# Filler products on the tensor engine in the opening of a two-block transformer kernel: 23 of 69 taken out

## The chip, the cores and the metric

The kernel runs on one core of a Trainium2 chip. The metric is the device time of one execution in microseconds (us), lower is better. Engines are called as in the profile: PE is the tensor engine's matmuls, PEld its weight loads, DVE the vector engine, ACT the scalar engine, POOL the GpSimd engine, SPq the queue from which the DMAs are issued. The "granted clock" of PE is 1.00 at 2.4 GHz and 0.50 at 1.2 GHz.

## The reference, cut to what matters

Two blocks of two layers each work on 256 tokens (the first block on 256 context tokens too) of width 1024. Each layer of the first block is modulated: a vector of 9 x 1024 numbers is computed from a condition vector and then scales and shifts the normed tokens before every sub-layer. The change lies before the very first sub-layer:

```python
mod_l = (jax.nn.silu(c) @ ada_w[i] + ada_b[i])[:, None, :]
sh1, sc1, g1, sh2, sc2, g2, sh3, sc3, g3 = jnp.split(mod_l, N_MOD, axis=-1)
x = x + 0.5 * g1 * swiglu(modulate(rms(x), sh1, sc1), pre_wi, pre_wo)
```

Only the first two parts, sh1 and sc1 (2 x 1024 numbers, for the latent and for the context condition), are needed before the first weight product of the feed-forward step. Everything behind that is the long rest: feed-forward, attention, and the second block.

## The kernel before, in words

**The stages.** The program is a list of stages, and each engine runs its part of each stage in the same order, held together by semaphores. The first stages are `statistics` (sum of squares of the tokens), `ada` (sh1 and sc1 on the tensor engine), `norm` (the modulated tokens, as a rounded high part `h_hi` and a rest `h_lo`), and the first feed-forward stage, which begins with `first_opening`.

**The ada stage.** The two weight parts come in eight pieces of 1 MB (512 rows by 512 columns each), one DMA each into a ring of four buffers `raw` (line 55, `RAWS = 4`). In `ada_step` (lines 923 to 941) a "row" step multiplies one piece by the condition, in 4 products of 512 columns that use 32 columns of the array each (line 935). After two pieces ACT copies the sums to `rows` (line 1415). After four pieces a "turn" step (line 940) brings the 1024 sums into the layout of the tokens, by 8 products of 2 columns. So `s.steps` holds ten steps: pieces 0 to 3, a turn, pieces 4 to 7, a turn. The first turn gives sh1, the second sc1; DVE adds the bias (line 2043) and one (line 2033).

**The filler.** `keep_awake(n)` (lines 956 to 959) multiplies a constant table of ones by itself, 128 columns, n times, into half of the bank `pm` that nobody reads. `ada` (lines 943 to 954) issues 28 of them before the first piece and then 5, 5, none (the square sums of line 787 stand there), 2, 2 (first turn), 5, 5, 5, 2, 10 (second turn) behind the ten steps. That is 69 calls. The profile counts each fp32 product twice (138 records at line 959, 8 per piece at line 935, 16 per turn at line 940).

**The loads.** SPq issues all loads in one order: a constant table, the tokens, the eight pieces, and then the weight units of the feed-forward step (2 DMAs of 512 KB each, all at line 706, in blocks of 512 bytes). Pieces 4 to 7 each wait until the piece that held their buffer has been multiplied; the units 0, 1, 2 and 3 wait in the same way for pieces 4, 5, 6 and 7:

```python
elif kind == "unit":
    sp.wait_ge(S["ada_done"], len(ada_units) - RAWS + n + 1)
```

**The first feed-forward products.** ACT rounds unit 0 to `w_hi` (line 1391), then makes `h_hi` of the first two of eight token chunks (line 1473), then rounds unit 1, then goes on with `h_hi`. DVE makes `full` (line 2102) and `h_lo` (line 2121) chunk by chunk. `first_opening` on PE takes a chunk as its `h_lo` comes: for the chunks 0 to 2 four products of unit 0 (lines 796 and 797), from chunk 3 on four of unit 0 and four of unit 1; then the products by the units' low parts (line 803), and the context tokens (lines 732 to 734).

Of the kernel before, what the change touches and what calls it, by code (L numbers as in the profile page):

```python
# [57 lines left out]
PER_MOD = (KC // ADA_K) * (D // ADA_COLS)  # L58
# [127 lines left out]
def build(nc, x_t, vecs, consts, positions, cond_rows, ada_first, ada_t, pre_wi, pre_wo, post_wi, post_wo, a_w_qkv, a_w_o, b_w_qkv, b_w_o,  # L186
# [413 lines left out]
    def con(name):  # L600
        if name in ANGLES:
            return angles[:, ANGLES.index(name), :]
        o, w = CON[name]
        return con_sb[:, o:o + w]
# [74 lines left out]
    with block:  # L679
# [36 lines left out]
        def _(pe):  # L716
# [63 lines left out]
            def square_sums(st, p):  # L780

                tok = st.parts[p]
                per = 0 if st.after is None else st.after.run.cols // P
                pe.wait_ge(S["square_added"], st.b["square_added"] + KC + 2 * per * p)
                if p:
                    pe.wait_ge(S["log_ready"], st.b["log_ready"] + p)
                pe.matmul(pm[:, 0, tok], con("ones"), square_sum[:, tok], start=True, stop=True).then_inc(S["square_summed"], 1)
# [135 lines left out]
            def ada_step(s, k):  # L923

                kind, j, bank_i, before = s.steps[k]
                o = ADA_BANKS[bank_i]
                if before is not None:
                    pe.wait_ge(S[before[0]], before[1])
                if kind == "row":
                    n = s.run.t0 + j  # L930
                    w, landing, count = raw_of("ada", n)
                    pe.wait_ge(landing, count)
                    for c in range(ADA_K):
                        quarter = slice(32 * c, 32 * (c + 1))
                        last = pe.matmul(o[quarter, :], cond[:, j % 2 * ADA_K + c, :], w[:, c * ADA_COLS:(c + 1) * ADA_COLS],
                                         start=j % 2 == 0, stop=j % 2 == 1)
                    last.then_inc(S["ada_done"], 1)
                    return
                for c in range(KC):
                    last = pe.matmul(o[:, 2 * c:2 * c + 2], rows[:, c * P:(c + 1) * P], con("fold"), start=True, stop=True)  # L940
                last.then_inc(S["ada_turned"], 1)

            def ada(s):
                pe.wait_ge(cond_ready, 1)
                pe.wait_ge(early_landed, 16)
                keep_awake(28)
                for k in range(len(s.steps)):
                    ada_step(s, k)
                    if k == 2:
                        square_sums(s.first, 0)  # L950
                    elif s.steps[k][0] == "turn":
                        keep_awake(10 if k + 1 == len(s.steps) else 2)
                    else:
                        keep_awake(2 if s.steps[k + 1][0] == "turn" else 5)

            def keep_awake(n):

                for _ in range(n):
                    pe.matmul(pm[:, 1, 0:P], con("ones"), con("ones"), start=True, stop=True)
# [400 lines left out]
            def branch_out(s):  # L1360
                waits_of(pe, s)
                sweep(pe, s.run, lambda u: dense(u, SEQ, x_of(s), s.ready))

            todo = dict(ada=ada, ffn_in=dense_run, proj=dense_run, heads=heads, values=values, diff=diff, soft=soft, pairs=pairs,
                        iw=iw, glu=dense_run, cc=cc, plain=plain, gates=gates, stick=stick,
                        branch=branch_out, conv_in=dense_run)
# [1682 lines left out]
```

## Time and profile before

| | |
|---|---|
| median of 3 runs | 2828.85 us |
| lowest and highest of them | 2827.34 and 2831.7 us |
| the profiled execution, its own time | 2830.01 us |
| its span, first to last instruction | 2827.9 us |
| PE busy | 2782.1 us, 98% of the span |
| mean granted clock of PE over the span | 0.998 |

The profile is of one execution. Its span is 2.1 us shorter than its time. Times in the views count from the start of the span. A busy PE is not PE at its peak, since the ends of pipelined matmuls are modelled; the pace is read from starts, or from the number of products in a stretch. The ada stage and the first products lie in the first 66 us.

### The profile page before, as it was taken

The page shows a single profiled execution, that of the slowest core. Times are in us where ns is not written, and L with a number is a line of the kernel's source. Part 1 is how long each engine was busy: PE and PEld are TensorE (multiplying, and loading weights), DVE is VectorE, ACT ScalarE, POOL GpSimd, SP SyncE. Part 2 cuts the span into 40 slices and gives each one's busy share as a digit, 9 for nine tenths or more (in the row PEclk, how much of TensorE's full clock was granted, in tenths as well). Part 3 has the DMA queues.
Part 4 walks back from the last instruction along what each step waited for, and adds up shares of the span by engine and source line. Part 5 has one row for each costly group of instructions (what it writes and reads, how often), then busy time and mean ns, then how long its engine had stood idle before and what let it go on. Part 6 is the DMA issues. An engine that isn't in the chain of part 4 may idle for free.

```text
span 2827.9 us, 43713 instructions
## 1 busy us (share of the span) xinstructions
PE 2782.1 (98%) x18332; PEld 2515.5 (89%) x18332; DVE 1994.0 (71%) x2863; ACT 1122.8 (40%) x1448; POOL 547.4 (19%) x408
## 2 busy tenths in 40 slices
PE   8999999989999999999999999999999999999999
PEld 7888897858888888888887999999999999999999
DVE  4767854386777858646577756988687788867866
ACT  4222234374212223122256435445553355455432
POOL 0100100000100101001000110798001129930000
PEclk9999999999999999999999999999999999999999
DMA  8656532202556635445331566554466675535665
GB/s 277 185 163 197 177 100 89 78 13 75 156 161 196 190 108 178 130 140 164 113 112 48 156 192 180 157 176 138 135 195 181 165 205 154 160 115 180 178 184 142
DMA packets 593171, 427.31 MB, mean 151 GB/s; under 512 B 16848, under 2 KB 571088, under 8 KB 592720
## 3 DMA queue, kind: packets, MB, share of 16 engines
q1 hardware_dynamic: 592976, 424.53, 50.7%
q8 instruction: 145, 2.38, 0.4%
q14 instruction: 50, 0.41, 0.0%
HBM read 423.43 MB, written 1.05 MB: 150 GB/s over the span
## 4 chain that ended last, share of the span: by engine, by line
PE 76%; POOL 13%; DVE 6%; DMA 2%; ACT 2%; issue 1%; SPq 0%; DVEq 0%; ACTq 0%; POOLq 0%
PE ps L732 22%; PE ps L733 22%; PE ps L734 21%; POOL cb_product L2919 7%; POOL cb_sum L2925 3%; DVE w_lo L1987 2%; ACT w_hi L1391 1%; DMA raw<-in_w_in 1%; PE ps L912 1%; PE ps L1056 1%; PE ps L1058 1%; PE ps L1057 1%; PE ps L913 1%; PE ps L914 1%; PE pm L1027 1%
## 5 line engine op out<-in xcount | busy, mean ns | idle before, releaser
L732 PE MATMUL ps<-h_hi,w_hi 128*128 128x256 f32 (+1 forms) x3488 | 1113.3, 319 | 7.3 <-DVE w_lo L1987 5.8
L733 PE MATMUL ps<-h_lo,w_hi 128*128 128x256 f32 (+1 forms) x3488 | 1105.4, 317 | 0.0
L734 PE MATMUL ps<-h_hi,w_lo 128*128 128x256 f32 (+1 forms) x3488 | 1105.3, 317 | 0.0
L1987 DVE TENSOR_TENSOR w_lo<-raw,w_hi 128x2048 fp32r<-128x2048 f32 (+2 forms) x376 | 813.4, 2164 | 231.2 <-ACT w_hi L1391 228.0
L1391 ACT CAST w_hi<-raw 128x2048 fp32r<-128x2048 f32 (+2 forms) x376 | 631.1, 1679 | 427.5 <-PE ps L734 299.8
L732 PEld LDWEIGHTS ps<-h_hi,w_hi 128*128 128x128 f32 x3488 | 665.5, 191 | 55.3 <-DVE w_lo L1987 8.3
L733 PEld LDWEIGHTS ps<-h_lo,w_hi 128*128 128x128 f32 x3488 | 665.8, 191 | 43.5 <-issue 0.2
L734 PEld LDWEIGHTS ps<-h_hi,w_lo 128*128 128x128 f32 x3488 | 665.7, 191 | 43.3
L2892 POOL TENSOR_TENSOR act_lo<-sil,act_hi 128x512 fp32r<-128x512 f32 (+1 forms) x132 | 164.9, 1249 | 1651.9 <-DVE act_hi L2262 1286.8
L732 PE MATMUL ps<-act_hi,w_hi 128*128 128x256 f32 (+1 forms) x1122 | 367.9, 328 | 0.7 <-DVE w_lo L1987 0.3
L733 PE MATMUL ps<-act_lo,w_hi 128*128 128x256 f32 (+1 forms) x1122 | 366.7, 327 | 0.0
L734 PE MATMUL ps<-act_hi,w_lo 128*128 128x256 f32 (+1 forms) x1122 | 366.6, 327 | 0.0
L2061 DVE SCALAR_TENSOR_TENSOR dot_t<-chunk_w,cond_all 128x1024 f32<-128x1024 f32 x256 | 310.4, 1258 | 6.4 <-DMA chunk_w<-in_ada_t 6.4
L1551 ACT ACTIVATE sil<-ps 128x512 f32<-128x512 f32 (+1 forms) x88 | 47.9, 544 | 557.9 <-PE ps L734 554.7
L732 PEld LDWEIGHTS ps<-act_hi,w_hi 128*128 128x128 f32 x1122 | 213.4, 190 | 20.3 <-DVE w_lo L1987 1.4
L733 PEld LDWEIGHTS ps<-act_lo,w_hi 128*128 128x128 f32 x1122 | 213.4, 190 | 18.1
L734 PEld LDWEIGHTS ps<-act_hi,w_lo 128*128 128x128 f32 x1122 | 213.4, 190 | 18.0
L2919 POOL TENSOR_SCALAR cb_product<-cb_in,vec_sb 128x256 f32<-128x256 f32 x120 | 195.1, 1636 | 5.9
L2159 DVE SCALAR_TENSOR_TENSOR xs<-ps,mod_sb,xs 128x256 f32<-128x256 f32 x136 | 60.5, 479 | 156.3 <-PE ps L734 156.3
L2260 DVE TENSOR_TENSOR sil<-sil,ps 128x512 f32<-128x512 f32 (+1 forms) x88 | 54.5, 619 | 142.4 <-ACT sil L1551 142.3
L2925 POOL TENSOR_TENSOR cb_sum<-cb_sum,cb_product 128x512 f32<-128x512 f32 x60 | 89.4, 1490 | 5.0
L1056 PE MATMUL ps<-w_hi,h_hi 128*128 128x256 f32 x288 | 82.8, 288 | 0.0
(312 smaller groups left out, 3178.8 us busy)
## 6 DMA issues: line engine op xcount, KB each, us to landing
chunk_w<-in_ada_t SPq DMA_DIRECT2D x128, 512.0 KB, 4.1
raw<-in_w_in SPq DMA_DIRECT2D x62, 1024.0 KB, 5.3
raw<-in_ffn_pre_wi SPq DMA_DIRECT2D x88, 512.0 KB, 5.3
raw<-in_ffn_post_wi SPq DMA_DIRECT2D x88, 512.0 KB, 5.2
raw<-in_ffn_pre_wo SPq DMA_DIRECT2D x32, 704.0 KB, 4.6
raw<-in_ffn_post_wo SPq DMA_DIRECT2D x32, 704.0 KB, 4.8
raw<-in_w_ffn_gate SPq DMA_DIRECT2D x44, 512.0 KB, 4.0
raw<-in_w_ffn_up SPq DMA_DIRECT2D x44, 512.0 KB, 5.3
```

The lines of the kernel that those rows point to most:

```text
L732: pe.matmul(o, hi, x_hi[:, k, tok], start=k == 0, stop=False)
L733: pe.matmul(o, hi, x_lo[:, k, tok], start=False, stop=False)
L734: return pe.matmul(o, weights(w_lo[u.low], u, k, m * P, P), x_hi[:, k, tok], start=False, stop=k == u.run.kc - 1)
L1056: pe.matmul(o, h_hi[:, k, tok], hi, start=k == 0, stop=False)
L1391: nc.scalar.copy(w_hi[u.slot][:, 0:n], whole[:, 0:n]).then_inc(hi_ready, 1)
L1987: nc.vector.tensor_tensor(w_lo[u.low][:, 0:n], whole[:, 0:n], w_hi[u.slot][:, 0:n].bitcast(F32), ALU.subtract).then_inc(lo_ready, 1)
L2061: nc.vector.scalar_tensor_tensor(dot_t[st], chunk_w[n % 2], 1.0, cond_all[:, st, :], ALU.mult, ALU.mult, accum_out=mod_sb[s.layer][:, at_f ...
L2159: last = nc.vector.scalar_tensor_tensor(xs[:, c, tok], o, mod_sb[layer][:, which * KC + c, st:st + 1], xs[:, c, tok], ALU.mult, ALU.add)
L2260: nc.vector.tensor_tensor(sil[:, r, 0:N], sil[:, r, 0:N], ps[u.slot][:, 1, 0:N], ALU.mult).then_inc(S[run.free], 1)
L2892: nc.gpsimd.tensor_tensor(o, whole, hi.bitcast(F32), ALU.subtract).then_inc(S[signal], 1)
L2919: ins = nc.gpsimd.tensor_scalar((product if w else dst)[:, c, :], x, weights_of(c, w), None, ALU.mult)
L2925: nc.gpsimd.tensor_tensor(dst[:, chunks, :], dst[:, chunks, :], product[:, chunks, :], ALU.add).then_inc(S[signal], 1)
```

## The change

The rule that says how many filler products stand behind a step is rewritten:

```diff
                     ada_step(s, k)
                     if k == 2:
                         square_sums(s.first, 0)
-                    elif s.steps[k][0] == "turn":
-                        keep_awake(10 if k + 1 == len(s.steps) else 2)
-                    else:
-                        keep_awake(2 if s.steps[k + 1][0] == "turn" else 5)
+                    elif k + 1 == len(s.steps):
+                        keep_awake(4)
+                    elif s.steps[k][0] == "row" and s.steps[k][1] + 1 < PER_MOD:
+                        keep_awake(5)
+                    elif s.steps[k + 1][0] == "turn":
+                        keep_awake(2)
```

`PER_MOD` is 4, the pieces of one part. Behind the ten steps there now stand 5, 5, the square sums, 2, 0, 0, 0, 0, 2 and 4 calls. The 28 before the first piece stay.

## Rows read from the trace of the kernel before

**Rows 1.** The page: busy time, then the chain that ended last

```profile
PE 2782.1 (98%) x18332; PEld 2515.5 (89%) x18332; DVE 1994.0 (71%) x2863; ACT 1122.8 (40%) x1448; POOL 547.4 (19%) x408
PE 76%; POOL 13%; DVE 6%; DMA 2%; ACT 2%; issue 1%; SPq 0%; DVEq 0%; ACTq 0%; POOLq 0%
```

**Rows 2.** Chain, 20 to 50 us: start us, length us, what

```profile
34.65 6.52 DMA raw<-in_ffn_pre_wi
41.19 1.90 ACT w_hi L1391
43.53 0.50 DVE h_lo L2121
```

**Rows 3.** Timeline of PE: start us, length us, operation, count [idle before]

```profile
23.89 1.07 PE L935 MATMUL ps<-raw,cond 128*32 128x512 f32 x8 [2.13 <-DMA raw<-in_ada_first]
...
27.47 0.69 PE L959 MATMUL pm<-con_sb 128*128 128x128 f32 x4
28.09 1.07 PE L935 MATMUL ps<-raw,cond 128*32 128x512 f32 x8
29.09 1.38 PE L959 MATMUL pm<-con_sb 128*128 128x128 f32 x10
30.40 1.07 PE L935 MATMUL ps<-raw,cond 128*32 128x512 f32 x8
...
32.70 1.07 PE L935 MATMUL ps<-raw,cond 128*32 128x512 f32 x8
...
35.01 1.07 PE L935 MATMUL ps<-raw,cond 128*32 128x512 f32 x8
...
36.78 1.95 PE L940 MATMUL ps<-con_sb,rows 128*128 128x2 f32 x16
38.59 3.97 PE L959 MATMUL pm<-con_sb 128*128 128x128 f32 x20
42.21 0.56 PE L796 MATMUL ps<-h_hi,w_hi 128*128 128x256 f32 x1
...
44.08 0.39 PE L796 MATMUL ps<-h_hi,w_hi 128*128 128x256 f32 x1 [0.44 <-DVE h_lo L2121]
```

**Rows 4.** Timelines of DVE and ACT, 38 to 45 us, columns as before

```profile
38.77 0.17 DVE L2043 TENSOR_TENSOR mod_sb<-ps,vec_sb 128x16 f32<-128x16 f32 x1 [10.88 <-PE ps L940]
...
39.90 0.90 ACT L1473 ACTIVATE h_hi<-full,mod_sb 128x256 fp32r<-128x256 f32 x2
41.19 1.90 ACT L1391 CAST w_hi<-raw 128x2048 fp32r<-128x2048 f32 x1 [0.39 <-DMA raw<-in_ffn_pre_wi]
```

**Rows 5.** Piece 5's issue; unit 1's; landing times of pieces 4 to 6, 7

```profile
18.06 0.37 SPq L706 DMA_DIRECT2D raw<-in_ada_first  x1
25.02 0.37 SPq L706 DMA_DIRECT2D raw<-in_ada_first  x1
31.52 3.08 SPq L706 DMA_DIRECT2D raw<-in_ffn_pre_wi  x1
...
raw<-in_ada_first SPq DMA_DIRECT2D x3, 1024.0 KB, 11.2
raw<-in_ada_first SPq DMA_DIRECT2D x1, 1024.0 KB, 9.7
```

**Rows 6.** Stretches: busy time of the engines, granted clock, DMA share, GB/s

```profile
35.00:36.00 1.00, 1.00 (x9) 0.16 (x8) 0.00 (x0) 0.00 (x0) 0.00 (x0) 1.00 0.78 209
37.00:38.00 1.00, 1.00 (x11) 1.00 (x10) 0.00 (x0) 0.00 (x0) 0.00 (x0) 1.00 0.63 174
...
8.70:39.30 30.60, 26.54 (x206) 17.57 (x205) 5.81 (x12) 9.03 (x15) 0.00 (x0) 1.00 1.04 361
39.35:42.70 3.35, 3.35 (x18) 3.35 (x17) 2.97 (x7) 2.96 (x4) 0.00 (x0) 0.50 1.04 300
```

**Rows 7.** PE near 2554 us: an idle stretch, then pace at either clock

```profile
2554.38 0.39 PE L732 MATMUL ps<-h_hi,w_hi 128*128 128x256 f32 x1 [2.73 <-DVE w_lo L1987]
...
2554.94:2558.34 3.40, 3.40 (x18) 3.40 (x17) 3.35 (x3) 0.00 (x0) 0.00 (x0) 0.50 0.54 172
2558.40:2561.80 3.40, 3.40 (x30) 3.40 (x30) 2.05 (x3) 1.91 (x1) 0.00 (x0) 1.00 0.00 0
```

**Rows 8.** All waits of PE from 45 to 564 us; filler pace

```profile
PE ps L796 <- DVE h_lo L2121: 0.2, 1, 0.2
...
4.80:8.30 3.50, 3.50 (x16) 3.50 (x17) 1.00 1.00 318
9.00:12.50 3.50, 3.50 (x34) 3.50 (x33) 1.00 1.05 400
```

## The prediction, made before the changed kernel was run

> **What bounds the kernel now.** I read the page first: PE is busy for 98% of the span and carries 76% of the chain [rows 1]. So what the opening does to the total is how much earlier or later PE begins its unbroken stream of products, provided nothing behind takes the shift back. I asked for PE's waits next: from 45 to 564 us there is one, of 0.2 us, at the very start [rows 8]. A shift of the stream passes on whole for 500 us, and I take it to pass on to the end, since the later stages hang on PE's products in turn.
>
> Then I asked what starts that stream. The timeline of PE shows it at 44.08 us, after 0.44 us of idling for `h_lo` [rows 3]. The eight products before that (chunks 0 and 1, from 42.21) are a prelude. The chain says what the stream waited for [rows 2]: the second DMA of unit 1, issued at 34.65 and landed at 41.17; ACT's rounding of unit 1, 1.90 us from 41.19; only then ACT's `h_hi` of chunk 2 and DVE's `h_lo` at 43.53. The filler behind the last turn, 3.97 us from 38.59 [rows 3], stands on no link of this. The reader should see that the wait that ends last at 44.08 is a landing, 0.39 us after ACT was free for it [rows 4].
>
> **The sum, part by part.** One filler call at full clock costs 0.26 us: the ten records from 29.09 end where piece 5 begins at 30.40, 1.31 us for five calls [rows 3]. At half clock it costs about twice that, 16 records in 3.5 us against 34 [rows 8].
>
> *Two calls behind the first turn, gone:* 27.47 to 28.09, 0.62 us. Piece 4 can start at 27.47 if it is there. The DMAs of pieces 4 to 6 took 11.2 us each, so piece 5, issued at 18.06, landed at 29.26, and its neighbours, read 2.71 us earlier and later, at 26.55 and 31.97 [rows 5]. Piece 4 is there. It ends near 28.5 in place of 29.1.
>
> *Fifteen calls behind pieces 4, 5 and 6, gone:* 3 x 1.31 = 3.9 us of PE time. But piece 5 lands at 29.26 (it started at 30.40), piece 6 at 31.97 (started 32.70), piece 7, issued at 25.02 with 9.7 us on the way, at 34.7 (started 35.01) [rows 3, 5]. PE waits for each in place of multiplying ones. Of 4.5 us removed, the last piece gains 0.3 us. The turn follows it, and DVE's bias (38.77) and the end of ACT's first two `h_hi` (40.80) come 0.3 us earlier [rows 4]. ACT then waits 0.7 us for unit 1 where it waited 0.4. Cost nothing, gain nothing, and the cover is that landing.
>
> *Does the landing move?* The units' DMAs wait for pieces 4, 5 and 6, and these end 0.5, 1.1 and 0.7 us earlier. Nothing is queued behind them on SPq that PE needs before 44 us but the units themselves. Unit 1's first issue started at 31.52 and stood for 3.08 us, to 34.60, just where piece 7 landed [rows 5]; the queue was full, not late, and an earlier start ends at the same place. The bound for a gain is what the DMA engines left unused: 0.22 us in 35 to 36 and 0.37 us in 37 to 38 [rows 6], 0.6 us together. The bound for a loss is unit 0's blocks getting between piece 7's, at most by the 0.5 us that they come earlier; that stays inside the 0.7 us of ACT's wait. I take nothing, because the issue row shows the full queue, and keep 0.6 us as the gain end.
>
> *Six calls behind the last turn, gone:* the filler ends near 39.4 at full clock in place of 42.56. Chunks 0 and 1 can start as their `h_lo` come, near 40.7 and 41.6, and are done by about 42.1; chunk 2 still comes at 44.02. Gain nothing.
>
> *What the filler held up:* the clock. It stood at 1.00 from 8.70 to 39.30 with PE busy for 26.5 of 30.6 us, among it an idle stretch of 2.13 us before piece 3, and fell to 0.50 from 39.35 to 42.70, directly after the stretch with the turn's two-column products. There PE worked without a pause at half clock, and the clock came back before the stream [rows 3, 6]. Now PE will do about 1 us of products between 39.4 and 44.08. The nearest row for what that does is at 2554 us: 2.73 us idle, then half clock over 3.40 us, in which 18 products ran where 30 run at full clock [rows 7]. That costs 3.40 x 12/30 = 1.36 us if all of it falls on the stream. The other end is 0: the half clock may be over by 44.08, as it was before, or lie on the prelude. Nothing in the trace says where it starts, so I take the middle, 0.7 us.
>
> *The rest of the diff* is Python, unrolled at build time. Sum: 0 + 0 + 0.7 = +0.7 us on the profiled execution's 2830.01 us, so 2830.7. The median of the three runs is 1.16 us below that execution, so 2829.6.
>
> **The rivals.** *No shift (28%).* The same chain, with the clock back in time or never down. For it: the half clock of before cost nothing, and 2.13 us of idling left the clock alone [rows 3, 6]. 2828.9 us.
>
> *A little faster (12%).* The earlier starts of the units' DMAs fill the unused 0.6 us, unit 1 lands 0.6 us earlier, and ACT is ready for it. Against it: the 3.08 us issue that ends with piece 7's landing [rows 5]. 2828.3 us.
>
> *Slower, by the clock among the pieces (13%).* From piece 4 on PE does 1.07 us of work in every 2.71 us and waits for a DMA in between; before, filler stood in all of these gaps. If the clock falls there and is at half through piece 7 and the second turn, piece 7 takes 1.0 us more and the turn 2.0 us more (its weight loads run at the filler's pace, and 16 records to 34 is a factor of 2.1) [rows 3, 8]. Less the 0.7 us that ACT waits for unit 1, the link is 2.3 us late, and 1.4 us at half clock behind it make 3.7 us: 2832.6 us. It decides once the turn ends over 0.7 us late. Two more stretches at half clock in the stream (2.7 us) would bring it to 6.4 us, 2835.3, over the bound for slower; I give that 4% of the 13. Against it stand the piece before 23.89, behind 2.13 us of idling, with no fall [rows 3, 6], and that PE at half clock is busy most of the time on the same pieces, after which it came back at 42.70.
> The Trainium skill speaks against the change here: "TensorE: Matmul & The Clock Gate", section "Loop structure matters more than you think", has it that a loop which waits for a DMA before each matmul runs at half clock. By that rule the pieces would all run so and the time would be this rival's, 2832.6 us; the trace agrees for the 2.73 us near 2554 us and not for the 2.13 us before piece 3.
>
> *The change doesn't do what it says.* By the conditions, steps 0 and 1 keep 5, step 3 and 8 keep 2, step 9 gets 4, the others nothing: 23 calls less. I give this nothing.
>
> **How the numbers follow.** Forecast 42%, no shift 28%, faster 12%, clock among the pieces 13%, and 5% for what I have not seen. The three runs of before alone span 2827.34 to 2831.7. The low end is the faster rival less the 1.5 us by which the lowest run lies under the median, 2826.8; the high end is the slower rival, 2832.6. About 0.2% of the time, 5.7 us, is what a measurement of this kernel can tell from no change. All cases but the longest clock case lie inside: slower 6% (4% and half of the unseen), faster 3%, the same 91%.
>
> **What would show it.** Line 959 has 92 records in place of 138. Pieces 5, 6 and 7 start at about 29.3, 32.0 and 34.75, each with idle time before it put down to `in_ada_first`. Unit 1's rounding still starts near 41.2 with ACT idle before it by about 0.7 us, and the product of chunk 2 near 44.1. The granted clock of the stretch 44 to 48 decides between forecast and no shift: below 1.00 and fewer than 8.3 products per us is the forecast. If unit 1's rounding starts before 40.9 the queue was not full and the faster rival holds. If the second turn lasts over 2.5 us the slower one does. A shift of the stream that PE makes up before 564 us would prove the first paragraph wrong.

## The result, and the profile after

The changed kernel takes 2835.62 us (median of 16 runs, 2833.36 to 2838.54), the kernel before beside it 2829.86 us (16 runs, 2827.28 to 2833.84). The ratio is 1.0019, 95% interval 1.0011 to 1.0027: slower by 5.8 us, 0.2%. The forecast was 2829.6 us and no difference, the range ended at 2832.6. The profiled execution took 2834.84 us, with a span of 2832.7 us, 4.8 us longer than before.

The page first, as [rows 1]:

```profile
PE 2782.6 (98%) x18286; PEld 2512.0 (89%) x18286; DVE 1993.6 (70%) x2863; ACT 1122.7 (40%) x1448; POOL 547.2 (19%) x408
PE 75%; POOL 13%; DVE 6%; DMA 3%; ACT 2%; issue 2%; SPq 0%; DVEq 0%; ACTq 0%; POOLq 0%
```

PE has 46 records fewer, the 23 calls, and is no less busy. The timeline of PE in the opening answers to [rows 3] (start us, length us, operation, count, idle before):

```profile
27.07 1.21 PE L935 MATMUL ps<-raw,cond 128*32 128x512 f32 x8
28.85 1.94 PE L935 MATMUL ps<-raw,cond 128*32 128x512 f32 x8 [0.57 <-DMA raw<-in_ada_first]
31.65 1.93 PE L935 MATMUL ps<-raw,cond 128*32 128x512 f32 x8 [0.87 <-DMA raw<-in_ada_first]
34.29 1.94 PE L935 MATMUL ps<-raw,cond 128*32 128x512 f32 x8 [0.70 <-DMA raw<-in_ada_first]
36.16 1.22 PE L961 MATMUL pm<-con_sb 128*128 128x128 f32 x4
37.17 3.41 PE L940 MATMUL ps<-con_sb,rows 128*128 128x2 f32 x16
40.45 2.05 PE L961 MATMUL pm<-con_sb 128*128 128x128 f32 x8
42.95 0.55 PE L796 MATMUL ps<-h_hi,w_hi 128*128 128x256 f32 x1 [0.46 <-DVE h_lo L2123]
...
45.42 0.39 PE L796 MATMUL ps<-h_hi,w_hi 128*128 128x256 f32 x1 [0.41 <-DVE h_lo L2123]
```

The pieces start when they land, as forecast, but the clock falls among them: a piece takes 1.94 us in place of 1.07 and the second turn 3.41 in place of 1.95. The stretches of the clock answer to [rows 6], ACT's and DVE's rows to [rows 4]:

```profile
11.00:27.80 16.80, 14.27 (x110) 8.73 (x108) 5.45 (x9) 6.64 (x12) 0.00 (x0) 1.00 1.05 388
27.90:44.90 17.00, 14.40 (x64) 8.46 (x60) 3.41 (x10) 6.23 (x8) 0.00 (x0) 0.50 1.08 328
```

```profile
40.62 0.17 DVE L2045 TENSOR_TENSOR mod_sb<-ps,vec_sb 128x16 f32<-128x16 f32 x1 [13.20 <-PE ps L940]
...
41.74 0.91 ACT L1475 ACTIVATE h_hi<-full,mod_sb 128x256 fp32r<-128x256 f32 x2 [2.00 <-DVE full L2104]
42.55 1.88 ACT L1393 CAST w_hi<-raw 128x2048 fp32r<-128x2048 f32 x1
```

ACT no longer waits for unit 1; unit 1 waits for ACT. Its rounding starts at 42.55 in place of 41.19, and the stream at 45.42 in place of 44.08: 1.34 us late. The clock is back at 44.9, just before it.

That is 1.34 of the 4.8 us by which the span grew. To find the rest I matched the two traces product by product on PE, from the end backwards, and took the difference of their starts:

| time in the kernel before, us | later in the changed kernel by, us |
|---|---|
| 45 to 345 | 1.35 |
| 370 to 1000 | 2.71 to 2.73 |
| 1060 to 1480 | 4.11 |
| 1600 | 5.16 |
| 1660 | 6.64 |
| 1780 | 7.15 |
| 2320 to 2500 | 7.93 |
| 2560 to the end | 4.73 to 4.87 |

The shift is handed on unchanged for 300 us and then grows in steps, the four largest of 1.0 to 1.5 us, far from anything that was edited.

The fall at 2554 us is time that the profile of the kernel before lost, not time that the change gained. PE's wait of 2.73 us there [rows 7] hangs on one load, in the chain of the kernel before (start us, length us, what):

```profile
2543.05 6.95 DMA raw<-in_w_in
```

In each of the 13 other profiles of this document that load takes 5.1 to 5.5 us, no half clock follows, and the kernel makes up 3.0 to 3.3 us on the kernel before; in the changed kernel the wait is 1.01 us. Only one profile of the kernel before was kept, so whether that kernel often loses these 3 us stays open. The shift of 4.7 us at the end is 7.9 less 3.2 of them.

The first step, in PE's waits from 45 to 564 us, as [rows 8]:

```profile
PE ps L732 <- POOL act_lo L2894: 1.1, 1, 1.1
PE ps L796 <- DVE h_lo L2123: 0.6, 2, 0.4
```

The wait of 1.1 us was not there. Followed back, in the changed kernel: PE waits at 353.53 for POOL's `act_lo`, POOL for DVE, and DVE for a chunk of the later modulation weights (line 691):

```profile
353.53 0.50 PE L732 MATMUL ps<-act_hi,w_hi 128*128 128x512 f32 x1 [1.07 <-POOL act_lo L2894]
```

```profile
346.97 1.23 DVE L2063 SCALAR_TENSOR_TENSOR dot_t<-chunk_w,cond_all 128x1024 f32<-128x1024 f32 x1 [2.95 <-DMA chunk_w<-in_ada_t]
```

The same load in the kernel before:

```profile
344.11 1.23 DVE L2061 SCALAR_TENSOR_TENSOR dot_t<-chunk_w,cond_all 128x1024 f32<-128x1024 f32 x1 [1.43 <-DMA chunk_w<-in_ada_t]
```

The load is issued 1.34 us later but lands 2.86 us later. The DMA view over its flight shows what was different. Changed, issue to landing (341.76 to 346.95), the last number of the row for `chunk_w` being us to landing:

```profile
q1 hardware_dynamic: 1469, 1.20, 78.2%
q8 instruction: 1, 0.02, 1.1%
...
chunk_w<-in_ada_t SPq DMA_DIRECT2D x1, 512.0 KB, 5.2
```

Before (340.42 to 344.09):

```profile
q1 hardware_dynamic: 655, 0.79, 74.0%
...
chunk_w<-in_ada_t SPq DMA_DIRECT2D x1, 512.0 KB, 3.7
```

In the changed kernel one 16 KB block of instructions (0.02 MB on queue 8, at 344.65 us) is fetched on the DMA engines while the load is on its way, and before there was none. The other large steps have the same shape, with a block at 1000.4 us (a load of 5.6 us against 4.2), at 1579.3 us (6.3 against 5.3) and at 1643.3 us (6.4 against 4.7).

Why would a block come later? In the kernel before two fetches in a plain stretch come at 188.0 and 216.4 us, and between them PE does 127 matmuls, each with its weight load:

```profile
188.00:216.40 28.40, 28.40 (x127) 23.54 (x126) 19.10 (x27) 5.37 (x4) 0.00 (x0) 1.00 0.65 200
```

So a block is PE's, some 256 of its instructions. The 23 calls were 92 instructions (46 matmuls, 46 weight loads). With them gone PE reaches every block boundary 46 matmuls further on in the work, 46 x 28.4/127 = 10.3 us later. The fetches, put on the clock of the kernel before (less the shift of PE at that place), stand at 331.8 and 360.5 before, and at 343.3 and 371.2 after, 11.5 and 10.7 us later. The Trainium skill ("Runtime: NRT & Kernel Launch", section "Instruction fetch mechanics") says that instructions are refilled in blocks of 16 KiB, 256 instructions each, by the sequencer's own DMA queue; the counts here agree. It adds that the cost of crossing a block is mostly hidden; no run here tests that for PE's own issue, but the loads beside it are another matter.

### The profile page after: what moved, and what is told of

The parts are those of the page before. It is cut to its first block, busy times and chain, and to the rows that moved or that the text cites. A ratio compares the mean times of both kernels' runs of the same rounds, so it can differ in the third digit from the quotient of the medians.

```text
span 2832.7 us, 43621 instructions
## 1 busy us (share of the span) xinstructions
PE 2782.6 (98%) x18286; PEld 2512.0 (89%) x18286; DVE 1993.6 (70%) x2863; ACT 1122.7 (40%) x1448; POOL 547.2 (19%) x408
## 4 chain that ended last, share of the span: by engine, by line
PE 75%; POOL 13%; DVE 6%; DMA 3%; ACT 2%; issue 2%; SPq 0%; DVEq 0%; ACTq 0%; POOLq 0%
PE ps L732 21%; PE ps L734 21%; PE ps L733 21%; POOL cb_product L2921 7%; POOL cb_sum L2927 3%; DVE w_lo L1989 2%; ACT w_hi L1393 1%; DMA raw<-in_ada_first 1%; DMA raw<-in_w_in 1%; PE ps L912 1%; PE ps L1058 1%; PE ps L1060 1%; PE ps L1059 1%; PE ps L914 1%; PE ps L913 1%
## 5 line engine op out<-in xcount | busy, mean ns | idle before, releaser
L732 PEld LDWEIGHTS ps<-act_hi,w_hi 128*128 128x128 f32 x1122 | 213.3, 190 | 24.4 <-POOL act_lo L2894 3.4
```

The lines of the kernel that those rows point to most:

```text
L732: pe.matmul(o, hi, x_hi[:, k, tok], start=k == 0, stop=False)
```

## The experiments

Three theories went into the first runs: the clock among the pieces (the slower rival of the prediction), the idle tail behind the last turn, and the position of the code. Most kernels have the rule replaced by a list of the ten counts behind the ten steps; in the diffs the minus line gives, in the same form, the counts of the kernel that it starts from. "Later part" below is the time from PE's first product at line 803, which ends the prelude and the first part of the stream, to PE's last, in the profiled execution: 2770.96 us before, 2774.38 changed. Both ends are starts of products. The start of that part is 51.32 before and 52.67 changed. Medians of a kernel are of 11 runs, those of the kernel before of the runs beside it on the same chip. A ratio and its 95% interval are as recorded, and need not be the quotient of the two medians. A profile is one of the 11 executions, and can lie some us from the median.

**Four calls in place of ten behind the last turn, alone.**

```diff
-                        keep_awake((5, 5, 0, 2, 2, 5, 5, 5, 2, 10)[k])
+                        keep_awake((5, 5, 0, 2, 2, 5, 5, 5, 2, 4)[k])
```

> The kernel before with one part of the change: 4 filler calls in place of 10 behind the last turn. Three theories. 'Among the pieces': the clock falls because PE idles between pieces 4 to 7, the second turn then runs at half clock and comes late; then this kernel is like the one before (about 2829.9 us, within 1.5) and its second turn still takes about 1.9 us. 'Tail': the idle stretch behind the last turn keeps the clock at half into the stream of products; then this kernel carries most of the 5.8 us (2834 to 2836) and the granted clock behind 44 us is below 1.00. 'Code position': every call taken out shifts the rest of the program on PE and the loads meet it differently; then it carries 6 of 23 calls' share, about +1.5 us, with the start of the stream unchanged.

2831.27 us against 2830.44, ratio 1.0002 (0.9993 to 1.0010). No theory of a large cost in the tail survives. The profile does show the clock at half well into the stream,

```profile
42.85:49.55 6.70, 5.95 (x26) 5.69 (x27) 5.89 (x14) 4.55 (x8) 0.00 (x0) 0.50 1.03 400
```

and the part from line 803 began at 54.22 us, 2.9 us late. But this kernel began badly too (half clock from 15.5 to 18.9 and 29.1 to 32.5, where all its filler stood), and the next but one shows the same with the tail whole.

**No calls behind pieces 4, 5 and 6, alone.**

```diff
-                        keep_awake((5, 5, 0, 2, 2, 5, 5, 5, 2, 10)[k])
+                        keep_awake((5, 5, 0, 2, 2, 0, 0, 0, 2, 10)[k])
```

> The kernel before with one part of the change: no filler calls behind pieces 4, 5 and 6 (15 calls less). 'Among the pieces': this is the part that costs, +3 to +6 us (2833 to 2836), piece 7 takes 1.9 us in place of 1.07 and the second turn 3.4 in place of 1.95. 'Tail': like before, within 1.5 us. 'Code position': 15 of 23 shares, +3.8 us, but with the start of the stream near 44.1 us.

2831.19 us against 2830.44, ratio 0.9999 (0.9990 to 1.0008). The turn does take 3.4 us, half clock from 32.7 to 42.9, and line 803 begins 1.0 us late (52.35). The forecast of the first theory, 3 to 6 us, is missed; that of the third, 3.8 us, as well, and with it the idea that the cost goes by shares of the calls. The later part is short, 2768.51 us, but the profiled execution, 2828.54 us, is the fastest of the 11.

**No calls behind the first turn, alone.**

```diff
-                        keep_awake((5, 5, 0, 2, 2, 5, 5, 5, 2, 10)[k])
+                        keep_awake((5, 5, 0, 2, 0, 5, 5, 5, 2, 10)[k])
```

> The kernel before with one part of the change: no filler calls behind the first turn (2 less). 'Among the pieces' and 'tail': no difference, within 1.5 us of before, since the filler behind piece 4 is there. A variant of 'among the pieces': the fall is decided at the first turn already (in the changed kernel the clock fell at 27.9 us, just behind it), then this kernel's granted clock falls near 28 us in the profile as well, and comes back sooner, since the filler behind pieces 4 to 6 keeps PE busy. 'Code position': +0.5 us.

2829.18 us against 2830.44, ratio 0.9995 (0.9986 to 1.0004). The clock did not fall near 28 us, so the variant of the theory misses. It fell later, with all the filler of before behind the pieces and the last turn:

```profile
44.55:51.25 6.70, 6.00 (x28) 6.00 (x29) 6.43 (x11) 2.46 (x6) 0.00 (x0) 0.50 1.01 399
```

28 products in 6.7 us, and line 803 at 54.73 us, 3.4 us late, in a kernel with one of the lowest medians of all (its profiled execution took 2832.14 us, 3.0 over the median). One profile of the opening is one draw: where the clock falls differs from execution to execution.

**The changed kernel with ten calls behind the last turn.**

```diff
-                        keep_awake((5, 5, 0, 2, 0, 0, 0, 0, 2, 4)[k])
+                        keep_awake((5, 5, 0, 2, 0, 0, 0, 0, 2, 10)[k])
```

> The changed kernel with 10 calls behind the last turn again. 'Among the pieces': nearly as slow as the changed kernel, 2833 to 2836 us, second turn 3.4 us long. 'Tail': back at 2830 us. 'Code position': 17 of 23 shares, +4.3 us, with the stream starting near 44.1 us.

2830.30 us against 2830.44, ratio 0.9997 (0.9988 to 1.0006). Six calls more and the 5.8 us are gone. Yet the six alone cost nothing (first run). Either the parts cost only together, or it is the number: 17 calls fewer is harmless and 23 is not. The later part is 2768.57 us, in an execution of 2828.43 us, 1.9 under the median.

The next four kernels tell these two apart, by calls at a place that is far from pieces 4 to 7 and the tail: the 28 ahead of the first piece.

**The changed kernel with 34 calls ahead, 17 fewer in all.**

```diff
-                keep_awake(28)
+                keep_awake(34)
```

> The changed kernel with 34 filler calls ahead of the first piece in place of 28: 17 calls fewer than before in all, the same number as in the kernel with ten calls behind the last turn, while pieces, turns and tail stay as changed. Theory 'code position': what cost 5.8 us is that with 23 calls fewer PE's instruction blocks of 16 KB are fetched some 10 us later against the stream of products, into loads that PE waits for (344.7, 1000.4, 1643.3 us in the changed kernel); with 17 fewer they come at 338.8 us on the clock of before again and miss them. Then this kernel is at 2829.5 to 2832 us, and the load issued near 341 us takes about 3.8 us in place of 5.2. Theory 'clock and tail together': the two parts cost only jointly, by the clock; then it is at 2834.5 to 2836.5 us like the changed kernel.

2829.73 us against 2830.31, ratio 0.9999 (0.9990 to 1.0008). The opening is the changed one in every row, with the turn at half clock,

```profile
33.97 1.94 PE L935 MATMUL ps<-raw,cond 128*32 128x512 f32 x8 [0.71 <-DMA raw<-in_ada_first]
35.84 1.23 PE L957 MATMUL pm<-con_sb 128*128 128x128 f32 x4
36.85 3.41 PE L940 MATMUL ps<-con_sb,rows 128*128 128x2 f32 x16
```

and the load near 341 us takes 4.1 us. The half clock even lasts longer, from 27.7 to 48.2 us, and line 803 begins at 53.31 us, 2.0 us later than before. The later part is 2768.65 us, 5.7 less than in the changed kernel, and the median is 5.6 us under the changed kernel's on this chip (2835.28 us, below), with no run of either among those of the other.

**The kernel before with 5 calls ahead, 23 fewer in all.**

```diff
-                keep_awake(28)
+                keep_awake(5)
```

> The kernel before with 5 filler calls ahead of the first piece in place of 28: all fillers of before around the pieces and turns stay, and 23 calls are gone, as in the change. 'Code position': from the stream's start to the end it takes as long as the changed kernel (from the first product at line 803 to the last some 2774 us, against 2768.5 to 2771.5 in the five others), there is PE idle time near 351 and 1007 us on the clock of before, and the time is 2833.5 to 2836.5 us. 'Clock and tail together': 2829 to 2832 us, unless the cold beginning makes the pieces late, which the start of the pieces would show.

2833.45 us against 2830.31, ratio 1.0009 (1.0000 to 1.0018), 0.05 us under the expected 2833.5 at the low end. The interval touches no difference, but the fastest of its 11 runs (2832.46) is slower than the slowest of the kernel with 34 ahead (2832.26). The opening is not quite that of before: with so few calls ahead the first piece runs at half clock (1.94 us), and line 803 begins at 51.75 us, 0.4 us late. Here the second turn runs at full clock,

```profile
37.70 1.95 PE L940 MATMUL ps<-con_sb,rows 128*128 128x2 f32 x16
```

and still the wait near 353 us and the late load are back, in PE's waits from 45 to 564 us and in the DMA view:

```profile
PE ps L732 <- POOL act_lo L2890: 1.2, 1, 1.2
...
chunk_w<-in_ada_t SPq DMA_DIRECT2D x1, 512.0 KB, 5.4
```

The later part is 2773.56 us. The same filler round the pieces as before, and 3.1 of the 5.0 us that the changed kernel is over the kernel before on this chip.

**The changed kernel with 21 calls ahead, 30 fewer in all.**

```diff
-                keep_awake(28)
+                keep_awake(21)
```

> The changed kernel with 21 filler calls ahead of the first piece: 30 calls fewer than before. 'Code position': the fetches move another 3.2 us back against the stream of products, near 346.5 us on the clock of before, behind the landing of the load near 345 that the changed kernel's fetch held up; the time changes again, with no change among pieces, turns and tail, by over 1 us in either direction (about 2831 to 2834 if the hits are narrow). 'Clock and tail together': the same as the changed kernel within 1 us, 2834.5 to 2836.5 us.

2832.11 us against 2830.31, ratio 1.0007 (0.9998 to 1.0015), 3.2 us under the changed kernel beside it. Seven calls less and it is faster. The time did move by over 1 us with pieces, turns and tail untouched, as the code position asks and the clock theory does not. The fetch stands at 345.5 us on the clock of before; the load has landed by then, in 3.6 us:

```profile
chunk_w<-in_ada_t SPq DMA_DIRECT2D x1, 512.0 KB, 3.6
```

**The changed kernel again.**

> The changed kernel, unchanged, on the chip and beside the runs of the three others: 2834.5 to 2836.5 us by every theory. 'Code position': a second profile has its fetch of 16 KB near 343.3 us on the clock of before and a late load there again, whatever its clock did in the opening. If the clock in the opening carries the cost, this profile's stream starts later than 45.4 us by as much as its span is above 2832.7 us.

2835.28 us against 2830.31, ratio 1.0018 (1.0009 to 1.0027). Its clock went another way, with half clock from 24.4 to 34.6 and from 38.1 to 48.3 and the turn between them at full clock (1.95 us), so that the clock theory's condition cannot be read plainly: the product of chunk 2 starts at 44.35 us, earlier than 45.42 and not later, but at half clock, and line 803 is at 52.92, 0.25 us after the first profile's, with the span 0.3 us longer. The fetch is at 342.7 us on the clock of before, the load takes 4.6 us, the later part 2774.45 us. PE's waits from 1000 to 1660 us:

```profile
PE ps L732 <- DVE w_lo L1985: 1.9, 2, 1.2
PE ps L732 <- POOL act_lo L2890: 1.9, 1, 1.9
```

**The kernel before with 12 calls ahead**, to take the good position together with the filler of before:

```diff
-                keep_awake(28)
+                keep_awake(12)
```

> A version that should beat both: all fillers of before around the pieces and turns, so the opening of before, and 12 calls in place of 28 ahead of the first piece, 16 calls fewer, which puts the instruction fetches where the kernels with 15 and 17 fewer had them. 'Code position': from the first product at line 803 to the last 2768.3 to 2769.3 us, against 2771.0 before, and 2827.5 to 2829.5 us in all, 1 to 3 us under before. If the position is only a matter of hits at the four or five loads seen, this is a fair gain; if it is at 2830 or above, the gain of the 15 and 17 was the luck of their profiles.

2830.39 us against 2831.09, ratio 0.9997 (0.9989 to 1.0006). The later part is 2770.03 us, over the 2769.3 expected, and no gain can be told. The 2768.5 of three profiles is in part the luck of single executions: two of the three ran 2.7 and 1.9 us under their kernel's median.

**The same, with unit 1 rounded behind the third chunk.**

```diff
-                        if (p, c) == (0, 1):
+                        if (p, c) == (0, 2):
                             split(Unit(*units[1]))
```

> The same, and ACT rounds unit 1 behind the third chunk of h_hi in place of behind the second. What the prediction held to start the stream, unit 1's landing, would then bind only from chunk 3 on: the product of chunk 2 starts near 42 us in place of 44 to 44.5, chunk 3 at most 0.4 us earlier than in the kernel beside it, and the time is lower by 0 to 0.5 us, which is less than the runs tell.

2829.18 us against 2831.09, ratio 0.9993 (0.9984 to 1.0002): the lowest beside its kernel before, and not told apart from it. Chunk 2 starts at 44.82 in place of 45.43 and waits 0.18 us in place of 0.90, as it no longer stands behind unit 1. It comes no earlier, with the second turn late (38.7 us) in both kernels:

```profile
44.82 0.39 PE L796 MATMUL ps<-h_hi,w_hi 128*128 128x256 f32 x1 [0.18 <-DVE h_lo L2119]
```

The expected 42 us took the turn to be early, and misses.

**The changed kernel with 31 and with 25 calls ahead, 20 and 26 fewer in all.**

```diff
-                keep_awake(28)
+                keep_awake(31)
```

> The changed kernel with 31 calls ahead of the first piece: 20 fewer than before, between the 17 that cost nothing and the 23 that cost some 5 us. 'Code position': the fetches stand half way, near 341, 996 and 1636.8 us on the clock of before, which is inside or just ahead of the loads issued at 340.4, 995.9 and 1635.3; 2831 to 2835 us, and from line 803 to the end 2770 to 2774.5. A smooth cost by the number of calls would give about 2832.5; a cost of hits can be anything between the two neighbours, and the loads' durations say which were hit.

> The changed kernel with 25 calls ahead of the first piece: 26 fewer than before, between 23 (2835.3) and 30 (2832.1). 'Code position': fetches near 344.5, 998.8 and 1639.5 us on the clock of before; the load of 340.4 has landed by then unless it is held up, those of 995.9 and 1635.3 are still on the way or just landing; 2832 to 2835 us, from line 803 to the end 2770.6 to 2774.5.

2832.30 and 2832.32 us against 2829.90, ratios 1.0006 (0.9998 to 1.0015) and 1.0006 (0.9997 to 1.0015). Both are 3 us under the changed kernel, though on another chip, and both later parts (2774.03 and 2771.96) are inside what was expected. In the first the load of 340.4 takes 4.6 us and the other two below are near normal; its later part holds a stretch of half clock at 1972.6 us as well, so it is a case between, not a clean one.

All kernels with the filler round the pieces as changed but for a different number ahead, and the one that swaps the two, side by side. The loads are those issued at 340.4, 995.9 and 1635.3 us on the clock of the kernel before, in us from issue to landing:

| kernel | calls fewer | median, us | three loads | later part, us |
|---|---|---|---|---|
| before | 0 | 2829.9 to 2831.1 | 3.7, 4.2, 4.7 | 2770.96 |
| changed, 34 ahead | 17 | 2829.73 | 4.1, 4.3, 5.1 | 2768.65 |
| changed, 31 ahead | 20 | 2832.30 | 4.6, 4.4, 5.0 | 2774.03 |
| changed | 23 | 2835.62 | 5.2, 5.6, 6.4 | 2774.38 |
| changed, again | 23 | 2835.28 | 4.6, 6.0, 6.4 | 2774.45 |
| before, 5 ahead | 23 | 2833.45 | 5.4, 4.9, 6.5 | 2773.56 |
| changed, 25 ahead | 26 | 2832.32 | 3.6, 3.9, 4.8 | 2771.96 |
| changed, 21 ahead | 30 | 2832.11 | 3.6, 3.6, 4.9 | 2770.62 |

The rows are of several chips. Against the kernel before on its own chip the medians are up by 2.4 us (20 fewer), 5.8 and 5.0 (the changed kernel), 2.4 (26) and 1.8 (30). The loss is largest at the number that the change happens to remove; of these only the changed kernel's is clear of its interval.

What a block beside a load does can be read across all 14 profiles, load by load. For the loads at the four large steps, "in flight" means that a block of queue 8 starts between 0.15 us before the load's issue and 3.3 us behind it. "PE later by" is by how much the difference of PE's starts to the kernel before grows across the place; numbers of profiles in brackets.

| load, issued before at | no block: load, us | PE later by | block in flight: load, us | PE later by |
|---|---|---|---|---|
| 340.4 | 3.6 to 4.1 (10) | 0.0 to 0.4 | 4.6 to 5.4 (4) | 0.8 to 1.5 |
| 995.9 | 3.5 to 4.3 (10) | -0.4 to 0.1 | 4.4 to 6.0 (4) | 0.2 to 1.8 |
| 1575.2 | 5.2 to 5.3 (8) | -0.05 to 0.0 | 5.9 to 6.7 (6) | 0.6 to 1.4 |
| 1635.3 | 4.7 to 4.9 (8) | 0.0 to 0.2 | 5.0 to 6.5 (6) | 0.1 to 1.6 |

The two groups do not overlap for any of the four loads, and PE's delay follows. It goes by the load and not by the kernel: with 26 and 30 calls fewer the blocks miss the loads at 340.4 and 995.9, which take their usual time, and hit the one at 1575.2 (6.2 and 6.7 us), where PE loses 0.9 and 1.4 us. Not every hit costs the same: at 1635.3 the three blocks that started within 0.6 us of the load's issue cost 0.1 to 0.2 us, the three that started 2.8 to 3.3 us behind it 1.5 to 1.6.

## Why the prediction was wrong

**The opening's chain: right.** PE now waits for each piece, and the 15 calls gave nothing. The landing of unit 1 did not move with the earlier issues: 41.17 before, 41.04 after (its first DMA stood in the queue for 3.3 us, where it had been 3.1). The filler behind the last turn stood on no link.

**The clock: among the rivals, with too small a chance.** The likeliest case put the half clock behind the last turn, on the stream, for 0.7 us. What the profiles show is the slower rival's first half: pieces at 1.94 us (forecast 1.0 us more, measured 0.9), turn at 3.4 us (2.0 more, measured 1.5; the factor of 2.1 came from a row whose clock column says 1.00 in both stretches [rows 8], where the turn itself shows 3.41 / 1.95 = 1.75), the link 1.36 us late (forecast 2.3). The clock was back before the stream in the first profile and at 48.3 us in the second. I gave that 13%, with the argument that no fall came behind 2.13 us of idling. That argument looked at the wrong thing. In the second profile the clock fell at 24.4 us, before the first place where the changed kernel issues anything else (behind the first turn), and in four kernels with all the filler behind pieces 4 to 6 it fell near the first turn as well (28.3 to 29.3 us). What differs is how soon it comes back: after 3.4 us in those four, after 10.2 to 20.5 us in seven of the eight profiles without that filler.

The Trainium skill ("TensorE: Matmul & The Clock Gate", section "Loop structure matters more than you think") has it that PE goes cold where a long wait for a DMA stands between every two matmuls; its example is a wait of 8 us. The prediction took it without the length. The waits before pieces 5 to 7 are 0.57 to 0.87 us in the changed kernel's first profile, and in the second the pieces 4 to 6 ran at half clock with no wait between them, so no run here tests that rule.

What the clock costs in the median is not settled. The changed kernel against the kernel before with 5 calls ahead, same number of calls and same chip, is 2835.28 - 2833.45 = 1.8 us (11 runs each, 2833.66 to 2838.87 and 2832.46 to 2835.02), and line 803 starts 0.9 to 1.2 us later in the two changed profiles; the rest is in the later part. With 17 calls fewer the same opening costs nothing that can be told (2829.73 against 2830.31 us).

**"A shift of the stream passes on whole", and nothing else changes: the step that failed.** The first half held for 300 us. What I left out is that taking instructions away is itself an edit of everything behind them. I counted the calls' time, their waits and the queues they touch, and wrote of the rest of the diff that it is Python, unrolled at build time, a term of nothing in the sum; the 92 instructions less on PE put every fetch of PE's instructions about 10 us later against the loads. In the profile the cost shows as four steps of 1.0 to 1.5 us, each where a load had a block of instructions fetched beside it. By the medians it is 2833.45 - 2830.31 = 3.1 us with the opening of before (23 calls fewer ahead against none) and 2835.28 - 2829.73 = 5.6 us with the opening of the change (23 fewer against 17). So of the 5.0 us on that chip the number of instructions carries at least some 3, and how the rest divides between it and the opening's clock stays open. No case of the forecast had a term of this kind, and the 5% for the unseen was too little beside it.

**What is shown and what is argued.** That the number of PE instructions ahead of the stream carries most of the loss, whatever the fillers round the pieces do, is shown by the pair of swaps (changed with 34 ahead is as fast as before, before with 5 ahead is slow) and by the runs on both sides of 23. That a fetched block beside a load holds the load up, and PE with it, is read from the table of four loads: no run moved a fetch without moving instructions, but single kernels have loads of both kinds, and they go by the block. The calls ahead are not a place quite without effect, as the late start of the first piece with 34 (15.28 us in place of 14.27) and its half clock with 5 show; and no run put all 23 calls back (51 ahead), which would be the plain test of the edit by itself. Which DMA engine carried the block and the late share of the load the profile does not say. And a load can be late without this pattern: the one at 2543.05 us in the kernel before took 6.95 us with a block 4.8 us behind its issue, and 5.4 us with a block 4.6 us behind it in the kernel without the two calls behind the first turn.

## What to carry to other kernels

Before taking a small edit's time for its cost, check what it does to the number of instructions on an engine that issues without a pause: here 127 matmuls with their weight loads lie between two fetched blocks, and the place of the blocks against loads that PE hangs on (1.5 us more of the load at 340.4 was 1.4 us of PE) is worth 3 to 5.6 us in 2830, by the medians of the two swaps. To judge a change of this size, run it once more with its instruction count put back at a place that does as little as possible; what goes away with it was not the edit. And read the clock in more than one profile, as one execution shows only one of the ways it can go.

## What the runs showed that was not expected

Two profiled executions of one kernel had different clocks in the opening: half clock from 27.9 to 44.9 us in one, from 24.4 to 34.6 and 38.1 to 48.3 us in the other, with spans of 2832.7 and 2833.0 us.

The clock fell where PE was not idle. In the kernel with five calls ahead PE had not waited since 25.03 us, and the clock was at half over

```profile
28.35:31.75 3.40, 3.40 (x18) 2.41 (x18) 0.00 (x0) 0.00 (x0) 0.00 (x0) 0.50 1.05 383
```

within 2 us behind the first turn's two-column products, as in [rows 6] behind the second turn.

One instruction block of 16 KB on the DMA engines goes with 0.7 to 1.8 us more for a load of 512 to 704 KB that is under way (the three loads of the table, the rows with 23 calls fewer against the kernel before).
